# Router logits from unscaled rows, expert choice tile by tile, and a first norm that turns one tile ahead

## The reference

```python
z = rmsnorm(x, g1) @ w_in            # columns for k, v, q, va, u
x = x + merge_out(...)               # mixer, then the output projection w_out
h = rmsnorm(x, g2)
pg = softmax(h @ r_g); gi = argmax(pg)            # one of 4 groups
le_sel = (h @ r_e).reshape(-1, 4, 4)[gi]          # the 4 experts of that group
tw, ti = top_k(softmax(le_sel), 2)                # two of them, with weights
x = x + sum over the two experts of gate * (silu(h @ w_gate) * (h @ w_up)) @ w_down
```

## Time and profile before

| | us |
|---|---|
| median of 3 runs | 1197.38 (1193.83 to 1199.59) |
| the profiled execution | 1199.92 |
| its span, first to last instruction | 1197.8 |
| TensorE matmuls busy | 1031.7 (86% of the span) |
| VectorE busy | 397.7 (33%) |
| granted TensorE clock, mean | 0.939 of 2.4 GHz |

### The profile page before, as it was taken

How to read it: one execution, slowest core, us unless ns; L and a number is a source line. 1 busy time by engine, 2 the same in 40 slices (tenths; PEclk the granted TensorE clock), 3 DMA queues, 4 the chain that set the end, 5 groups by cost and what they waited for, 6 DMA issues and landing times.

```text
span 1197.8 us, 12156 instructions
## 1 busy us (share of the span) xinstructions
PE 1031.7 (86%) x4388; PEld 525.0 (44%) x4388; DVE 397.7 (33%) x916; ACT 242.8 (20%) x495; POOL 208.6 (17%) x287
## 2 busy tenths in 40 slices
PE   4999999779986999999629999998799869999970
PEld 2434464455433544444214434544554335444430
DVE  2402124453226454111053031244632364541104
ACT  2111445420000111111112013554300001111110
POOL 1323113211001121211212131031210011212110
PEclk9999999879997999999959999999899979999995
DMA  9405032411052878898374050142210438789936
GB/s 357 160 17 219 1 106 76 141 37 71 36 193 93 299 285 334 336 339 302 132 266 177 0 219 0 56 127 106 71 71 36 193 111 297 290 312 336 336 133 214
DMA packets 42865, 206.08 MB, mean 172 GB/s; under 512 B 9392, under 2 KB 9520, under 8 KB 26160
## 3 DMA queue, kind: packets, MB, share of 16 engines
q1 hardware_dynamic: 20464, 142.31, 32.2%
q0 software_dynamic: 18928, 50.61, 12.3%
q10 hardware_dynamic: 3408, 12.32, 2.9%
HBM read 188.95 MB, written 33.03 MB: 185 GB/s over the span
## 4 chain that ended last, share of the span: by engine, by line
PE 75%; DVE 12%; DMA 5%; issue 3%; ACT 2%; POOL 1%; ACTq 0%; SPq 0%; POOLq 0%; DVEq 0%
PE ps L588 70%; PE ps L586 6%; DMA y_rows<-hn,isca 2%; DVE cat L1492 1%; DMA hT<-h_rows,igat 1%; DVE st L1330 1%; DMA cat<-y_rows 1%; DVE x L1626 1%; DMA x<-in_xp 1%; DVE hT L1212 1%; DVE hT L1593 0%; DVE ring L1342 0%; DVE tmp L1358 0%; DVE o_sb L1350 0%; DVE kva L1296 0%
## 5 line engine op out<-in xcount | busy, mean ns | idle before, releaser
L588 PE MATMUL ps<-ring,hT 128*128 128x512 f32 (+1 forms) x1184 | 507.4, 604 | 10.5 <-ACT ring L1078 3.7
L588 PEld LDWEIGHTS ps<-ring,hT 128*128 128x128 f32 (+1 forms) x1184 | 209.5, 188 | 268.0 <-issue 255.3
L588 PE MATMUL ps<-ring,cat 128*128 128x512 f32 (+1 forms) x592 | 248.0, 593 | 3.4 <-ACT hn L1132 2.4
L588 PEld LDWEIGHTS ps<-ring,cat 128*128 128x128 f32 (+1 forms) x592 | 101.6, 184 | 119.7 <-issue 116.9
L1593 DVE TENSOR_TENSOR hT<-ps,par 128x512 f32<-128x512 f32 x68 | 44.0, 686 | 197.0 <-PE ps L586 196.4
L524 POOL DMA_INDIRECT y_rows<-hn,isca x34 | 34.2, 1005 | 316.5 <-ACT hn L1132 270.5
L425 POOL TENSOR_SCALAR st<-st 128x1 f32<-128x1 f32 (+3 forms) x60 | 13.7, 228 | 353.5 <-ACT sqj L984 115.4
L588 PE MATMUL ps<-hT,ring 128*128 128x512 f32 (+1 forms) x256 | 71.8, 437 | 0.3 <-ACT cat L1028 0.3
L427 POOL TENSOR_TENSOR st<-st,half 128x1 f32<-128x1 f32 (+3 forms) x60 | 63.1, 1051 | 11.4 <-POOL st L425 10.5
L1330 DVE TENSOR_REDUCE st<-ps 128x2 f32<-128x256 f32 (+3 forms) x32 | 26.3, 823 | 114.5 <-PE ps L588 114.4
L1132 ACT COPY hn<-ps 128x1024 f32<-128x1024 f32 x34 | 34.4, 1012 | 141.7 <-PE ps L588 141.7
(11 more groups left out here) (210 smaller groups left out, 889.5 us busy)
## 6 DMA issues: line engine op xcount, KB each, us to landing
ring<-in_w SPq DMA_DIRECT2D x130, 1024.0 KB, 6.9
kc<-in_ck POOLq DMA_DIRECT2D x32, 256.0 KB, 3.7
vc<-in_cv POOLq DMA_DIRECT2D x32, 256.0 KB, 3.2
h_rows<-qk ACTq DMA_DIRECT2D x10, 512.0 KB, 2.6
qk<-y_rows POOLq DMA_DIRECT2D x8, 512.0 KB, 5.7
cat<-y_rows ACTq DMA_DIRECT2D x8, 512.0 KB, 8.6
y_rows<-vc POOLq DMA_DIRECT2D x5, 512.0 KB, 5.8
x<-in_xp SPq DMA_DIRECT2D x4, 512.0 KB, 10.6
```

The lines of the kernel that those rows point to most:

```text
L588: ins = pe.matmul(out, lhsT, rhs, start=start, stop=stop, skip_group_check=loose)
```

## The change

On TensorE the first norm turns only tile 0 ahead of the k columns, and tile t + 1 inside tile t, behind the step k = KD - 3 (the sixth of eight). On VectorE in layer 0 each tile is scaled and multiplied before the next.

For the router TensorE turns x itself, not the scaled rows, once VectorE has added the projection. Logits are made tile by tile with the 128 tokens standing and the router's 20 columns moving: those of tiles 0 and 1 behind the projections of tiles 2 and 3, those of tiles 2 and 3 inside the sample's projection, those of tile 4 behind it. VectorE chooses experts tile by tile (`chosen`), and multiplies the logits by the root later, in `logits_down`. The first group of indices is split in two, and `logits_down` comes behind the multiply of expert 0's rows. The scaled rows are still stored for the gathers.

```diff
-        GROUPS = [range(0, 2), range(2, 4), range(4, 8), range(8, 12), range(12, 16)]
+        GROUPS = [range(0, 1), range(1, 2), range(2, 4), range(4, 8), range(8, 12), range(12, 16)]
-        INDEX_AT = {0: 2, 1: 3, 2: 4, 5: 5, 7: 6}
+        INDEX_AT = {0: 3, 1: 4, 2: 5, 5: 6, 7: 7}
...
-                rows = hn2[:, t, :] if stage == "h2" else hn[:, t % 2, :]
+                rows = x[:, t, :] if stage == "x" else hn[:, t % 2, :]
...
-                            for j in [0, 1] if t == 0 else [t + 1] if t + 1 < NT else []:
-                                turn_rows("h1", j, dve_s.at("hn1", j))
+                            if t == 0:
+                                turn_rows("h1", 0, dve_s.at("hn1", 0))
...
+                            if c == 0 and k == KD - 3:
+                                turn_rows("h1", t + 1, dve_s.at("hn1", t + 1))
...
                 def sample_out():
                     claim("S0")
                     for k in range(KD):
+                        if k == HALF:
+                            turn_rows("x", TP - 1, read["S1"].at("y", 1, TP - 1))
+                            logits(TP - 2)
+                        if k == KD - 2:
+                            logits(TP - 1)
...
+                def logits(t):
+                    claim("O")
+                    for hf in range(2):
+                        pe.wait_ge(*read[f"T{hf}"].at("x", t, hf))
+                    for k in range(KD):
+                        mm(bank("O")[:, t * NR:(t + 1) * NR], hT[:, k, t * P:(t + 1) * P], par[:, PAR["router"]][:, k * NR:(k + 1) * NR],
+                           start=(k == 0), stop=(k == KD - 1), inc=full["O"].inc("logits", t) if k == KD - 1 else None)
...
+                    out_rows(t)
                     if t >= 1:
-                        turn_rows("h2", t - 1, dve_s.at("hn2", t - 1))
+                        turn_rows("x", t - 1, read["S1"].at("y", 1, t - 1))
+                    if t >= 2:
+                        logits(t - 2)
...
+                sample_out()
+                turn_rows("x", TP, read["S0"].at("y", 0, TP))
+                logits(TP)
                 for t in range(NT + 1):
+                    token_ranks(t)
...
-                act.wait_ge(*full["F"].at("logitsT"))
-                nc.scalar.copy(o_sb[0:NR, 0, :], bank("F")[0:NR, :]).then_inc(*read["F"].inc("logitsT"))
...
-                    norm_rows("h1", "rs1", "g1")
+                    scaled, turned = norm_tile("h1", "rs1", "g1")
+                    for t in range(NT):
+                        scaled(t)
+                        turned(t)
...
+                for t in range(NT):
                     if t < TP:
                         add_out(0, t)
-                    if t >= 1:
+                    if 1 <= t < TP:
                         scaled(t - 1)
                     if t < TP:
                         add_out(1, t)
-                    elif t == TP:
-                        add_sample_out()
                     if t >= 1:
                         turned(t - 1)
                     if t < 2:
                         head_turned(TP - 1 + t)
+                    if t >= 2:
+                        chosen(t - 2)
+                scaled(TP - 1)
+                chosen(TP - 1)
+                add_sample_out()
+                turned(TP)
+                scaled(TP)
+                chosen(TP)
...
                 def logits_down():
+                    link(vec.tensor_tensor(lg[:, :, :], lg[:, :, :], wide(stat["rs"], NT, NR), ALU.mult))
...
                 main_group(0)
-                logits_down()
                 main_group(1)
+                main_group(2)
                 in_turned(0, ("m", 0))
+                logits_down()
```

More of the change, by code:

```diff
@@ L253, in program @@
         M = sb("M", [P, NT * E], BF16)
-        placed = cat_cols[:, 3840:4240].rearrange("p (i n) -> p i n", i=5)
-        gates = cat_cols[:, 4240:4320].rearrange("p (t e) -> p t e", t=NT)
+        placed = o_sb[:, 0, 0:400].rearrange("p (i n) -> p i n", i=5)
+        gates = o_sb[:, 0, 400:480].rearrange("p (t e) -> p t e", t=NT)
         igat = sb("igat", [P, E + EXTRA + 2], mybir.dt.uint32)
@@ L831, in sample_out, with token_ranks @@
                         pending.append((piece_used, ()))
+                def logits(t):
[5 more added lines that the diff above has]
+                           start=(k == 0), stop=(k == KD - 1), inc=full["O"].inc("logits", t) if k == KD - 1 else None)
+                def token_ranks(t):
+                    pe.wait_ge(*dve_s.at("M", t if t < NT else TP))
+                    if t == 0:
+                        claim("I")
+                    for j in range(min(t + 1, NT)):
+                        mm(bank("I")[:, t * E:(t + 1) * E], c16[:, B_BEFORE if j == t else B_ONES], M[:, j * E:(j + 1) * E],
+                           start=(j == 0), stop=(j == min(t, NT - 1)), inc=full["I"].inc("ranks") if (t == NT and j == NT - 1) else None)
                 for t in range(NT):
@@ L835, in _ @@
                     pe.wait_ge(*read[OT[t]].at("oT", t))
[L836 to L839, removed]
+                    if t == TP:
+                        break
+                    out_rows(t)
                     if t >= 1:
-                        turn_rows("h2", t - 1, dve_s.at("hn2", t - 1))
+                        turn_rows("x", t - 1, read["S1"].at("y", 1, t - 1))
+                    if t >= 2:
+                        logits(t - 2)
                     if t < 2:
                         turn_out(TP - 1 + t)
[L847 to L870, removed]
+                sample_out()
+                turn_rows("x", TP, read["S0"].at("y", 0, TP))
+                logits(TP)
                 for t in range(NT + 1):
-                    for j in range(min(t + 1, NT)):
-                        mm(bank("I")[:, t * E:(t + 1) * E], c16[:, B_BEFORE if j == t else B_ONES], M[:, j * E:(j + 1) * E],
-                           start=(j == 0), stop=(j == min(t, NT - 1)), inc=full["I"].inc("ranks") if (t == NT and j == NT - 1) else None)
+                    token_ranks(t)
                 def index_rows(g):
@@ L933, in _ @@
                 index_rows(1)
+                index_rows(2)
                 turn_in(0, ("m", 0), hs_in[0].at("hs", "m", 0))
@@ L1209, in turned @@
                     for hf in range(2):
-                        dve.wait_ge(*full[f"T{hf}"].at(stage, t, hf))
+                        dve.wait_ge(*full[f"T{hf}"].at("x" if stage == "h2" else stage, t, hf))
                         g = par[:, PAR[gain]][:, hf * HALF:(hf + 1) * HALF].unsqueeze(2).to_broadcast([P, HALF, P])
                         vec.tensor_tensor(hT[:, hf * HALF:(hf + 1) * HALF, t * P:(t + 1) * P],
-                                          bank(f"T{hf}").rearrange("p (j t) -> p j t", j=HALF), g, ALU.mult).then_inc(*read[f"T{hf}"].inc(stage, t, hf))
+                                          bank(f"T{hf}").rearrange("p (j t) -> p j t", j=HALF), g, ALU.mult).then_inc(*read[f"T{hf}"].inc("x" if stage == "h2" else stage, t, hf))
                 return scaled, turned
[L1217 to L1221, removed]
-                    if t >= 1:
-                        turned(t - 1)
             def groups(ap, n, w):
@@ L1429, in _ @@
                 scaled, turned = norm_tile("h2", "rs2", "g2")
-                for t in range(NT + 1):
+                flat = placed[:, :, :]
+                selA, selB, R, win, work = (flat[:, i, :] for i in range(5))
+                ex = stat["ex"].rearrange("p (n j) -> p n j", j=EG)
+                lgg, lge = lg[:, :, 0:G], lg[:, :, G:20].rearrange("p t (g j) -> p t g j", g=G)
+                first = c32[:, C_FIRST][:, 0:EG * EG].rearrange("p (j i) -> p j i", j=EG).unsqueeze(1).to_broadcast([P, 1 + G, EG, EG])
@@ L1600, in _ @@
                 main_group(0)
+                main_group(1)
+                main_group(2)
+                in_turned(0, ("m", 0))
                 logits_down()
-                main_group(1)
-                in_turned(0, ("m", 0))
                 for n in range(E):
@@ L1606, in _ @@
                         g = INDEX_AT[n]
-                        (main_group if g < 5 else extra_group)(g)
+                        (main_group if g < 6 else extra_group)(g)
                     if n == 3:
```

30 lines of the change are left out of this document (added).

## The result

The changed kernel takes 1211.97 us (median of 7 runs, 1206.34 to 1214.12), the kernel before 1197.71 beside it (7 runs). The ratio is 1.0121, with a 95% interval of 1.0093 to 1.0148: slower by 14 us, between 11 and 18. The profiled execution took 1214.08 (span 1212.0, mean granted clock 0.933 against 0.939).

What follows compares the result with a forecast made beforehand. TensorE is three quarters of the chain that ended last. Starts +1.4 and +7.0, router stage +0.3 and +1.0 sum to +9.7: 1209.6, or 1207 in terms of the median; own range 1203 to 1211, wide range 1197 to 1216.

Steps and rivals of the forecast that it cites:

- rival (b): Sample's projection: the logits' short instructions let the clock fall inside it, +3.4 to +7 over both layers, 1212; chance 0.21.
- Starts, position of v: Start of the v columns: layer 0 at 51.7, a gain of 0.3; layer 1 at 662.8 instead of 657.5, +5.35.
- The clock in the gaps: Idle gaps of 6.5 and 5 us ahead of v: TensorE's clock falls, 1.7 each, ends 0 and 3.4.
- Router and choice: Projection to first expert: the rows' store replaces the choice on the path, +0.3 in layer 0, +1.0 in layer 1.
- The price of 9.0: Last rows' store, beside 4 MB of weights: takes 9.0 us to land, against 2.6 alone.
- Sum: Whole kernel: 1.4 + 7.0 + 0.3 + 1.0 = +9.7, giving 1209.6, or 1207 in terms of the median.
- (a): Gaps and last store: clock holds and store lands in 6 us or less, +2 to +3, 1200; chance 0.22.
- (c): Start of v: VectorE's stretch behind turning 4 does not hold bank S0; -11, 1186; chance 0.07.

Runs made afterwards that it cites:

- experiment 3: Changed kernel with VectorE's sums of squares of k tiles 0 and 1 ahead of its last multiply of the first norm: 1191.72 us, ratio 0.9949.
- experiment 6: Changed kernel with tile 4 turned behind the second k step of tile 3 instead of the sixth: 1200.84 us, ratio 1.0036.
- experiment 4: Changed kernel with tile 3's row store issued ahead of the square of the sample's tile: 1210.50 us, ratio 1.0109.
- experiment 2: Kernel before with the first norm by tiles alone: 1208.85 us, ratio 1.0098.
- experiment 5: Kernel before, old router kept, with the first norm by tiles and the early sums of k tiles 0 and 1: 1190.14 us, ratio 0.9958.
- experiment 7: Kernel before with only the sums of k tiles 0 and 1 ahead of VectorE's last multiply: 1193.82 us, ratio 0.9960.
- experiment 8: Changed kernel with the early sums of k tiles 0 and 1, and weights behind the projection held until the last rows are stored: 1194.56 us, ratio 0.9990.

## Why the prediction was right, point by point

The forecast was slower by 9.7 us, 1207; measured were 1212 and +14.3. Direction, place and mechanism hold; the size is a third too low. The clock term was too small, and 3 to 5 us stand in none of its terms. The wide range, 1197 to 1216, held the result; my own range, 1203 to 1211, just did not, and the room above it had been left for rival (b), whose cause did not occur. That part is luck.

**Starts, position of v.** Predicted for layer 0: -0.3. Measured: 54.05 - 51.99 = +2.06, of which 2.49 are the later landing of the parameters, so -0.4. All of the head start that one tile's turning gives is lost at bank S0, as the chain through VectorE said. Predicted for layer 1: +5.35; measured 663.39 - 657.48 = +5.9, less 0.25 by which the layer began late, 5.7. Experiments 3 and 6 confirm the cause from both sides: take VectorE's sum out of the chain and the gaps go; turn tile 4 3.4 us earlier and they shrink by 3.4.

**The clock in the gaps, the mis-sized term.** Predicted 1.7 for each, 3.4 together. Measured, by how far ScalarE's first reading of v slips beyond 7.17 us from the start of v: 2.5 and 1.6 in the changed kernel's profile, 3.0 and 2.1 in that of experiment 4, which has the same norm, 2.9 and 3.0 in experiment 2. So the same gaps cost 4.1, 5.1 and 5.9. The stretch that I priced them by the earlier trace rows ran at half clock for 3.4 us; the dense work behind the new gaps did so for 3.2 to 6.1. It was the wrong row: only 1.58 us of idling stood right ahead of it, while behind the gap of 4.16 us, which I named as the sign that the clock falls, the kernel before ran at half clock from 236.4 to 243.3, 6.8 us. "Twice that", which I kept as an end of the range, bounds all three profiles. What the Trainium skill says in TensorE: Matmul & The Clock Gate, section HAM oscillation, that long waits between bursts are each paid again as warm-up, agrees with both gaps of the changed kernel (6.45 and 5.10 us, 1.2 GHz behind each). The gaps of 3.02 and 1.67 us in experiment 6, behind which the clock stayed at 1.00, show that not every idle stretch is paid.

Experiment 2 closes on these terms: +0.4 for v in layer 0 (54.58 - 51.99, less 2.18 for the parameters), +4.95 for layer 1 (661.88 - 657.48, and the layer began 0.55 ahead), 5.9 of clock, 11.3 together; measured 11.4 (8.9 to 14.6).

**Router and choice.** Predicted +0.3 and +1.0; measured -0.56 and +0.75. The steps: choice to the end of `rows_of` 2.84 us a tile (2.8 predicted), the sample's adds end at 352.67 (354.1; the layer runs 0.9 ahead here), index at 364.2 (363.6), because the sample's turning and logits ran at half clock (the logits took 3.57 instead of 1.93 us); last store issued at 356.1 (357.3), landed in 8.2 and 8.6 (9.0). The later index and the earlier landing make a tie in layer 0, where the store was to decide; in layer 1 it does, and in experiment 4 it does in both layers (in layer 0 the index stood at 368.27, the landing at 370.4, the gather at 371.52). The price of 9.0 came from the row, and it was better than the packet-by-packet rule of DMA: Bandwidth & Descriptors, section Queues, rings and completion order, in the Trainium skill, which gave about half: with the store of tile 3 out of the way it still took 9.1 and 8.8.

**Sum.** By the traces -0.4 + 2.5 + 5.7 + 1.6 + 0.2 = +9.6, but the medians say 14.3 (11 to 18). With the 5.9 us of clock of experiment 2 in place of 4.1 it would be 11.4. The mean granted clock of the runs speaks to the rest: 0.933 over the changed kernel's seven, 0.942 over the 35 of the kernel before in the second set, a lack of 0.008, of which the two stretches behind the gaps (some 10 us at half clock, with the end of the gaps) make 0.004. Over those 35 runs, time falls 0.89 us for each 0.001 of mean clock (correlation -0.94), so the other 0.004 is worth some 3.7 us. That is argued, not shown. In the changed kernel's profile the experts' stages are 3.9 us longer than before, but among kernels with one and the same router they differ nearly as much: layer 0's took 248.2 to 250.4 us in the five profiles with the new router and 248.1 to 249.4 in the four with the old one, layer 1's 228.1 to 229.6 and 227.3 to 229.7. Why the changed kernel has more half clock elsewhere is open.

**Rivals.** (a) fell on both counts: the clock didn't hold, the store didn't land in 6 us. (b) gave 1212, the measured number, by a cause that did not occur: the clock fell at 352 in layer 0 and at 967 in layer 1, behind the sample's projection, not within it. (c) fell with experiment 3: the bank is held by VectorE's order, and released at the end of k once the sums go first. A number that fits is no evidence for its mechanism.

## What to carry to other kernels

Before letting an engine start earlier, follow the resource it will need next. Here a bank was released by a sum that stood behind unrelated work in VectorE's program order, and everything won at the front came back as idle time, with the clock on top. Two short instructions moved ahead of one (1.4 us of work) changed a loss of 14 us into a gain of 6. Of the kernels here, those of experiments 3, 5 and 7 are faster than the kernel before, and the times don't tell them apart; experiment 7 is the smallest edit of the three.

When a transfer is slow beside others, ask which transfer takes its place beside them: beside the same 4 MB of weights the store loses 6 us, most of which the choice of experts covered, or the gather of scattered rows 2.2 to 3.9, which nothing covered.

## What the runs showed of the hardware that I had not expected

The spread of one kernel's times goes with its mean clock. The 35 runs of the kernel before go from 1190.95 (mean clock 0.948) to 1205.49 (0.934), with a correlation of -0.94. In the profiles, half-clock stretches of 10 us and more in attention stood at 260 (before), at 871 (changed), at 257 and 861 both (experiment 7); in the other seven none there was longer than 6.8. So two single profiles may differ by 5 us or more in a stage that no edit touches, and where a few us are at stake, the stage is to be compared from its own start.

The parameters' load, the first thing that the norm waits for, lands early or 2 to 3 us later: the first scaling stood at 8.38 to 8.48 in five profiles (before, experiments 3, 6, 7, 8) and at 10.30 to 11.48 in the other five, with the same issues ahead of it. In the changed kernel that was 2.5 us of the difference between the profiles.
